# A three-block transformer kernel: in the first mixer, part of the shift row summed on VectorE, biases added by one-row products, constants loaded later

## The chip, the cores and the metric

The kernel is one program on one core of a Trainium2 chip. The metric is the device time in microseconds of one execution, as the median of several.

## The reference

Three different blocks are applied to x, 512 rows of 1024 numbers. The change lies in the start of the first one, which is, cut to what matters:

```python
mod = jax.nn.silu(c) @ w_ada + b_ada                     # 1024 -> 6 * 1024
shift1, scale1, gate1, shift2, scale2, gate2 = split(mod, 6)
h = rms_norm(x, norm1_w) * (1.0 + scale1) + shift1
proj = h @ w_in                                          # q, k, v, conv parts, index parts
...                                                      # selected attention, short convolution
x = x + gate1 * (y_mix @ w_out)
h2 = rms_norm(x, norm2_w) * (1.0 + scale2) + shift2
x = x + gate2 * peer_ffn(h2, ...)
```

The second block is a hybrid mixer with a mixture of experts, the third a hybrid attention layer; neither is touched.

## The kernel before

`first_mixer` does everything of the first block up to h2. The modulation has twelve half rows j of 512 columns (two for each of the six vectors), in the order `ADA_ORDER`: j = 0, 1 are scale1, j = 2, 3 are shift1, the others come later.

**Half rows 0 to 3** are products on TensorE (L661). The stationary operand is a column of silu(c) spread over 128 columns, the moving one a 128x512 part of w_ada, so each of the 128 rows of the PSUM bank `side[j % 2]` holds the same modulation row. Eight parts (k) make a half row; the parts of one half row come in two transfers of 1 MB (`ada_first`, semaphores `ada1_in`, eight in all). VectorE then adds the bias, which a broadcast transfer has put into `mod1` (L704 and L705 for scale1, with norm1_w; L708 for shift1).

**The rows.** ScalarE sums the squares of x (L754). VectorE multiplies the rows by the root and by scale1 (L714, four 128-row tiles) into `hn`, adds shift1 (L738), and TensorE transposes each tile in two halves of four 128x128 blocks (L774). ScalarE copies each half as its high part (L764), VectorE subtracts it for the low part (L743). After the eighth (`h_low` at 8) the weight products may start.

**Weight products.** `pieces` are the 128-column pieces of w_in (512 KB each). SP loads them into three buffers `raw` (L784), ScalarE rounds the high part (L813) and VectorE forms the low part (L821, `low_done`). TensorE makes 24 products of 512 columns a piece (L863), in eight groups k of three.

**Half rows 4 to 11** need pieces of 256 KB (`w_ada_later`, L647), through two buffers `ada_raw`; each piece q is multiplied by its column of silu(c) and accumulated on VectorE (L691 for the first of eight, L694 for the others, `ada_used`); a load waits until the piece two before it is used. One product with a matrix of ones (L672) then sums over the 128 rows, and VectorE adds the bias (L704, L705, L708).

**The index scores** of the attention (L1014 on TensorE, L1024 on ScalarE, L1036 and L1039 on VectorE, two buffers between each pair) start once six pieces of w_in are through; then VectorE selects the keys (L1050, L1055). The softmax lanes follow (L1095 to L1139), the output projection and h2.

**Order.** On each engine several Python generators yield between steps, and `weave_by` runs them in the order that `FIRST_ORDER` gives, written out as text: "c22" is 22 steps of the third program. Every engine executes its queue in order. For "sync" the programs are a `loads`, b `weights_in` and c `ada_in`; for "tensor" a `ada_tensor`, b `rows_tensor`, c `products`, e `rel_tensor`; for "scalar" a `rows_scalar`, b `rounded`; for "vector" a `ada_vector`, b `rows_vector`, c `rests`, f `rel_vector`. One step of `products` is one group of three products, eight make a piece; one step of `ada_vector` is one accumulation or the output after eight.

```python
def weave_by(order, *programs):
    for program in programs:
        next(program, None)
    for part in order.split():
        for _ in range(int(part[1:] or 1)):
            next(programs[ord(part[0]) - ord("a")], None)
```

`consts` is one 128-row tile of constants; its first 256 columns are the identity (`C["ident"]`) and the ones (`C["ones"]`).

## Time and profile before

| | us |
|---|---|
| median of 3 runs | 3362.2 |
| lowest and highest | 3358.63 and 3362.36 |
| profiled execution, its own time | 3367.17 |
| its span | 3365.4 |
| TensorE busy | 3012.6 (90%) |
| VectorE busy | 2430.1 (72%) |
| ScalarE busy | 1392.1 (41%) |
| GpSimd busy | 713.0 (21%) |

The span runs from the first instruction to the last of the profiled execution; its own time is what the same clock as that of the runs gave for it. Busy times are shares of the span. PE is TensorE, PEld its weight loads, DVE VectorE, ACT ScalarE, SPq the queue of SyncE that issues transfers. A matrix product in plain fp32 appears as two records. Ends of matmul records are modelled, so the distance between starts tells more than a duration.

### The profile page before, as it was taken

Reading aid. Unit: us, or ns where it says so; the run is one execution under the profiler, and the core shown is the slowest. Engines: PE = TensorE matmul, PEld = TensorE weight load, DVE = VectorE, ACT = ScalarE, POOL = GpSimd, SP = SyncE. Lnnn points to the kernel's source line nnn. Section 1 sums busy time; section 2 is a strip of 40 time slices with the busy share of each in tenths; the row PEclk is TensorE's granted clock in tenths of the full one; section 3 lists DMA queues with packets and bytes.
Section 4 is the critical chain, followed back from the end, with each engine's and each line's share of the span. In section 5 each row is a group of like instructions: output and inputs, shape, how many; then the busy total and the mean of one; then the engine's idle time right before and its main releaser. Section 6 shows DMA issues by size and latency. Waiting matters only on the chain. (4 is left out here: it accounts for less than half of the span.)

```text
span 3365.4 us, 35225 instructions
## 1 busy us (share of the span) xinstructions
PE 3012.6 (90%) x11968; PEld 1988.2 (59%) x11968; DVE 2430.1 (72%) x4830; ACT 1392.1 (41%) x2332; POOL 713.0 (21%) x583
## 2 busy tenths in 40 slices
PE   7999988887788777777789999999899999969999
PEld 4676633333333333333357898777788888857777
DVE  4888678777777777777759765555789888964665
ACT  2344222222222222222234333444588888853764
POOL 0000144444444444444410000000121222100000
PEclk9998989999988999999899999999999999989999
DMA  7423499999999999999962111343899999931112
GB/s 295 138 76 101 178 374 415 417 408 420 418 407 421 421 408 417 417 419 409 418 256 82 59 56 45 101 170 108 322 363 375 373 369 375 371 125 63 57 45 76
DMA packets 163767, 905.93 MB, mean 269 GB/s; under 512 B 27137, under 2 KB 27649, under 8 KB 71810
## 3 DMA queue, kind: packets, MB, share of 16 engines
q0 software_dynamic: 84000, 549.52, 39.8%
q1 hardware_dynamic: 79586, 354.11, 28.8%
q8 instruction: 100, 1.64, 0.2%
q14 instruction: 81, 0.66, 0.1%
HBM read 896.71 MB, written 31.99 MB: 276 GB/s over the span
## 5 line engine op out<-in xcount | busy, mean ns | idle before, releaser
L256 PE MATMUL peer_acc<-peer_uv,peer_diag 128*128 128x512 f32 x1952 | 959.3, 643 | 257.0 <-ACT peer_diag L308 254.6
L256 PEld LDWEIGHTS peer_acc<-peer_uv,peer_diag 128*128 128x128 f32 x1952 | 389.4, 205 | 806.2 <-issue 459.6
L435 DVE CUSTOM_DVE_ANT_0 peer_uv<-peer_uv,firsts_h 128x1024 f32<-128x1024 f32 x512 | 626.8, 1226 | 321.0 <-DMA peer_uv<-in_peer_uv,peer_experts 319.6
L213 POOL DMA_INDIRECT peer_uv<-in_peer_uv,peer_experts x512 | 590.2, 1153 | 1117.3 <-PE peer_acc L256 684.6
L3146 DVE TENSOR_TENSOR slotted_low<-slotted_raw,slotted_high 128x2048 fp32r<-128x2048 f32 x192 | 434.2, 2288 | 64.3 <-ACT slotted_high L3091 64.1
L3091 ACT ACTIVATE slotted_high<-slotted_raw 128x2048 fp32r<-128x2048 f32 x192 | 365.7, 1920 | 58.4 <-PE slotted_h L3044 47.8
L308 ACT ACTIVATE peer_diag<-all_consts,peer_weights 128x128 f32<-128x128 f32 x512 | 165.1, 390 | 313.6 <-DVE peer_weights L416 305.6
L299 ACT ACTIVATE peer_act_in<-peer_act_in 128x4 f32<-128x4 f32 (+2 forms) x131 | 26.8, 205 | 628.5 <-DVE peer_act_in L435 628.5
L3044 PE MATMUL slotted_h<-slotted_high,slotted_xT_high 128*128 128x512 f32 x512 | 203.1, 397 | 0.6 <-DVE slotted_xT_low L3153 0.6
L3044 PE MATMUL slotted_h<-slotted_high,slotted_xT_low 128*128 128x512 f32 x512 | 200.2, 391 | 0.0
L3044 PE MATMUL slotted_h<-slotted_low,slotted_xT_high 128*128 128x512 f32 x512 | 199.6, 390 | 0.0
L1821 PE MATMUL mixers_acc<-mixers_xT_high,mixers_high 128*128 128x512 f32 x448 | 192.0, 429 | 3.2 <-DVE mixers_low L1842 3.2
L1821 PE MATMUL mixers_acc<-mixers_xT_low,mixers_high 128*128 128x512 f32 x448 | 176.0, 393 | 0.0
L1821 PE MATMUL mixers_acc<-mixers_xT_high,mixers_low 128*128 128x512 f32 x448 | 175.5, 392 | 0.0
L2911 POOL MEMSET slotted_xg<- 128x1024 f32 x1 | 1.0, 952 | 639.4 <-POOLq L3317 639.4
L3006 POOL DMA_INDIRECT results<-slotted_ob,slotted_rows_out x32 | 32.3, 1009 | 451.9 <-ACT slotted_ob L3118 451.9
L1842 DVE TENSOR_TENSOR mixers_low<-mixers_raw,mixers_high 128x1024 fp32r<-128x1024 f32 (+1 forms) x77 | 93.1, 1209 | 40.9 <-ACT mixers_high L1835 40.1
L1835 ACT ACTIVATE mixers_high<-mixers_raw 128x1024 fp32r<-128x1024 f32 (+1 forms) x77 | 80.6, 1046 | 101.0 <-PE mixers_acc L1821 76.2
L3044 PEld LDWEIGHTS slotted_h<-slotted_high,slotted_xT_low 128*128 128x128 f32 x512 | 96.1, 188 | 21.1
L3044 PEld LDWEIGHTS slotted_h<-slotted_high,slotted_xT_high 128*128 128x128 f32 x512 | 96.1, 188 | 20.9 <-issue 0.7
L3044 PEld LDWEIGHTS slotted_h<-slotted_low,slotted_xT_high 128*128 128x128 f32 x512 | 96.3, 188 | 19.0
L863 PE MATMUL firsts_acc<-firsts_hT_high,firsts_high 128*128 128x512 f32 (+1 forms) x240 | 105.4, 439 | 1.8 <-DVE firsts_hT_low L743 1.8
(786 smaller groups left out, 5694.2 us busy)
## 6 DMA issues: line engine op xcount, KB each, us to landing
slotted_raw<-in_moe_w SPq DMA_DIRECT2D x192, 1024.0 KB, 7.3
mixers_raw<-in_w_in SPq DMA_DIRECT2D x56, 512.0 KB, 3.3
firsts_ada_raw<-in_w_ada_later SPq DMA_DIRECT2D x64, 256.0 KB, 2.7
third_raw<-in_w_in SPq DMA_DIRECT2D x30, 512.0 KB, 3.3
firsts_raw<-in_w_in SPq DMA_DIRECT2D x28, 512.0 KB, 3.5
firsts_ada_first<-in_w_ada_first SPq DMA_DIRECT2D x8, 1024.0 KB, 18.0
peer_uv<-in_peer_uv,peer_experts POOLq DMA_INDIRECT x512, 11.3
ffn_w_raw<-in_peer_wq SPq DMA_DIRECT2D x10, 512.0 KB, 8.4
```

The costliest lines, as they stand in the source:

```text
L213: pool.indirect_dma_start(uv[:, n % R, :, :].rearrange("p a d -> p (a d)"), None, A["peer_uv"], bass.IndirectOffsetOnAxis(ap=experts[:, si ...
L256: mm = nc.tensor.matmul(acc[t % 2][j][:, :], diag[:, n % 4, :], uv[:, n % R, 1, j * BANK:(j + 1) * BANK], start=(n == first), stop=(m == E ...
L308: nc.scalar.activation(diag[:, n % 4, :], C["ident"], ACT.Copy, scale=weights[:, side, i:i + 1])\
L435: nc.vector.tensor_tensor_reduce(uv[:, n % R, 0, :], uv[:, n % R, 0, :], h2[:, t, :], 1.0, 0.0, ALU.mult, ALU.add, act_in[:, side, i:i + 1 ...
L863: mm = nc.tensor.matmul(bank[rows, :], b, a, start=(k == 0 and r == 0), stop=(k == KD - 1 and r == 2))
L1821: mm = nc.tensor.matmul(bank[:, :], b, a, start=(k == 0 and r == 0), stop=(k == piece["kb"] - 1 and r == 2))
L1835: nc.scalar.activation(high[:, p % 2, 0:size], raw[:, p % RAW, 0:size], ACT.Copy).then_inc(high_done, 1)
L1842: nc.vector.tensor_tensor(low[:, p % 2, 0:size], raw[:, p % RAW, 0:size], high[:, p % 2, 0:size].bitcast(F32), ALU.subtract).then_inc(low_ ...
L3006: pool.indirect_dma_start(results, bass.IndirectOffsetOnAxis(ap=rows_out[:, e:e + 1], axis=0), ob[:, e % 2, :], None, bounds_check=2 * L - ...
L3044: mm = nc.tensor.matmul(ps_h[i // 2][:, :], a, b, start=(k == 0 and r == 0), stop=(k == KD - 1 and r == 2))
L3091: nc.scalar.activation(high[:, p % RING, :], raw[:, p % RAW, :], ACT.Copy).then_inc(high_done, 1)
L3146: nc.vector.tensor_tensor(low[:, p % RING, :], raw[:, p % RAW, :], high[:, p % RING, :].bitcast(F32), ALU.subtract).then_inc(low_done, 1)
```

## The change

Half rows 0 to 3 get their bias from a product with one row of ones as the stationary operand and the bias row as the moving one (`bias_row`, 8 KB), so the 1 MB broadcast into `mod1` is gone, and each output is one VectorE operation. Of half row 2 the first four parts are multiplied and summed on VectorE (`SUMMED`), and one product with ones adds the sum. Only the first 256 columns of the constants are loaded early, the others after the first weight pieces. Weight pieces 0 to 2 are all loaded behind the modulation pieces; before, piece 0 was first and 1 and 2 came behind later loads. `idle_products` multiplies ones with the identity into a bank that the next transposes overwrite: six before each tile, eight before the first weight product. The low part of weight piece 0 moves behind the first two row additions. The accumulations for half rows 4 to 6 all move behind the rows phase, and their ones products (L672) from 2, 24 and 45 groups of weight products to 20, 36 and 49.

```python
def idle_products(nc, C, bank, n):
    for _ in range(n):
        nc.tensor.matmul(bank[:, 0:P], C["ones"], C["ident"], start=True, stop=True)
```

```diff
--- before.py
+++ after.py
@@ -525,6 +525,7 @@
         acc_first, acc_last = arena.at(152 * KB + 128, "acc_first", [P, 2, BANK]), arena.at(0, "acc_last", [P, 2, BANK])
         ada_raw, tsq = arena.at(164 * KB + 128, "ada_raw", [P, 2, BANK]), arena.at(168 * KB + 128, "tsq", [P, 4, P])
         norm_row = arena.at(170 * KB + 128, "norm_row", [P, D])
+        bias_row = arena.at(156 * KB + 128, "bias_row", [P, 2 * D])
         w1_at = {2: 136, 3: 144, 0: 152, 1: 160}
         w1 = {kp: (arena.at(a * KB, f"w1_high{kp}", [P, 2, BANK], F32R), arena.at((a + 4) * KB, f"w1_low{kp}", [P, 2, BANK], F32R))
               for kp, a in w1_at.items()}
@@ -598,6 +599,8 @@
         c_ready, ada_done, ada_used, ada_out, gate2_out = (st.sem(n) for n in ("c_ready", "ada_done", "ada_used", "ada_out",
                                                                                "gate2_out"))
         ada_chain, eps_ready = st.sem("ada_chain"), st.sem("eps_ready")
+        square_in, bias_in, shift_used = st.sem("square_in"), st.sem("bias_in"), st.sem("shift_used")
+        SQUARE, SUMMED = 2 * P, 4
         FIRST = 32
 
         def ada_key(q):
@@ -605,6 +608,9 @@
 
         def ada_acc(j):
             return (acc_first if j < 4 + FIRST // 8 else acc_last)[:, j % 2, :]
+
+        def tile_of_bias(j):
+            return slice(COLS[j], COLS[j] + BANK)
 
         def mod_row(j):
             half = slice(BANK * (j % 2), BANK * (j % 2) + BANK)
@@ -619,13 +625,13 @@
                 j, kh = divmod(n, 2)
                 sp_queue.dma_start(ada_first[:, n], A["w_ada_first"][j, kh]).then_inc(ada1_in[n], 16)
                 if n == 0:
+                    sp_queue.dma_start(C["all"][:, 0:SQUARE], A["consts"][:, 0:SQUARE]).then_inc(square_in, 16)
+                    sp_queue.dma_start(bias_row[0:1, :], A["b_ada"][:, 0:2 * D]).then_inc(bias_in, 16)
                     sp_queue.dma_start(norm_row[:, :], A["norm1_w"].broadcast_to([P, D])).then_inc(rows_in, 16)
-                    sp_queue.dma_start(mod1[:, :, :], A["b_ada"][:, 0:2 * D].rearrange("o (a n) -> o a n", a=2)
-                                       .broadcast_to([P, 2, D])).then_inc(rows_in, 16)
                 if 1 <= n <= 4:
                     sp_queue.dma_start(x[:, n - 1, :], A["x"][tile(n - 1), :]).then_inc(x_in[n - 1], 16)
-            sp_queue.dma_start(C["all"], A["consts"]).then_inc(consts_in, 16)
             yield -60.0
+            sp_queue.dma_start(C["all"][:, SQUARE:], A["consts"][:, SQUARE:]).then_inc(consts_in, 16)
             for dst, name in ((cw[:, :, :], "conv_w_col"), (cb[:, :], "conv_b_col"), (cgain[:, :], "conv_norm_col"),
                               (qk_gain[:, :], "qk_norm_cols")):
                 sp_queue.dma_start(dst, A[name]).then_inc(small_in, 16)
@@ -655,12 +661,20 @@
             for j in range(4):
                 if j >= 2:
                     pe.wait_ge(ada_out, j - 1)
-                for k in range(KD):
+                direct = range(SUMMED if j == 2 else 0, KD)
+                for k in direct:
                     if k % 4 == 0:
                         pe.wait_ge(ada1_in[2 * j + k // 4], 16)
-                    mm = nc.tensor.matmul(side[j % 2][:, :], c_col[:, k:k + 1].broadcast_to([P, P]),
-                                          ada_first[:, 2 * j + k // 4, k % 4, :], start=(k == 0), stop=(k == KD - 1))
-                mm.then_inc(ada_done, 1)
+                    nc.tensor.matmul(side[j % 2][:, :], c_col[:, k:k + 1].broadcast_to([P, P]),
+                                     ada_first[:, 2 * j + k // 4, k % 4, :], start=(k == direct[0]), stop=False)
+                if j == 2:
+                    pe.wait_ge(shift_used, SUMMED)
+                    nc.tensor.matmul(side[0][:, :], C["ones"], ada_acc(2), start=False, stop=False)
+                if j == 0:
+                    pe.wait_ge(square_in, 16)
+                    pe.wait_ge(bias_in, 16)
+                nc.tensor.matmul(side[j % 2][:, :], C["ones"][0:1, :], bias_row[0:1, tile_of_bias(j)], start=False, stop=True)\
+                  .then_inc(ada_done, 1)
             for j in range(4, N_ADA):
                 yield ada_key(8 * (j - 3) - 1) + 1.5
                 if j == 4:
@@ -678,7 +692,8 @@
             for j in range(N_ADA):
                 if j < 4:
                     yield -190.0
-                    dve.wait_ge(rows_in, 32)
+                    if j == 0:
+                        dve.wait_ge(rows_in, 16)
                 else:
                     for k in range(KD):
                         q = 8 * (j - 4) + k
@@ -698,7 +713,12 @@
                     dve.wait_ge(mod_in, 64)
                 dve.wait_ge(ada_done, j + 1)
                 dst, bank = mod_row(j), side[j % 2][:, :]
-                if j < 2 or j in (6, 7):
+                if j < 2:
+                    nc.vector.scalar_tensor_tensor(dst, bank, 1.0, norm_row[:, BANK * j:BANK * j + BANK], ALU.add, ALU.mult)\
+                      .then_inc(ada_out, 1)
+                elif j < 4:
+                    nc.vector.tensor_copy(dst, bank).then_inc(ada_out, 1)
+                elif j in (6, 7):
                     if j == 6:
                         dve.wait_ge(norm2_in, 16)
                     chain(nc.vector.scalar_tensor_tensor(dst, bank, 1.0, dst, ALU.add, ALU.add))
@@ -707,6 +727,16 @@
                 else:
                     nc.vector.tensor_tensor(dst, bank, dst, ALU.add).then_inc(ada_out, 1)
                 if j == 1:
+                    dve.wait_ge(c_ready, 1)
+                    dve.wait_ge(ada1_in[4], 16)
+                    for k in range(SUMMED):
+                        part = ada_first[:, 4, k, :]
+                        if k == 0:
+                            ins = nc.vector.tensor_scalar(ada_acc(2), part, c_col[:, 0:1], None, ALU.mult)
+                        else:
+                            dve.wait_ge(shift_used, k)
+                            ins = nc.vector.scalar_tensor_tensor(ada_acc(2), part, c_col[:, k:k + 1], ada_acc(2), ALU.mult, ALU.add)
+                        ins.then_inc(shift_used, 1)
                     dve.wait_ge(rooted, 1)
                     chain(nc.vector.reciprocal(sums[:, :], sums[:, :]))
                     dve.wait_ge(ada_out, 2)
@@ -767,8 +797,8 @@
             for n in range(2 * NT):
                 t, half = divmod(n, 2)
                 yield row_key(t, 6) + 0.5 * half
-                if n == 0:
-                    pe.wait_ge(consts_in, 16)
+                if half == 0:
+                    idle_products(nc, C, all_banks[n], 6)
                 pe.wait_ge(rows_normed, t + 1)
                 for b in range(4):
                     tr = nc.tensor.transpose(all_banks[n][:, tile(b)], hn[:, t, tile(4 * half + b)], C["ident"])
@@ -828,7 +858,10 @@
                 size = piece["kb"] * piece["w"]
                 wh, wl = (b[:, p % 2, 0:size].rearrange("p (k n) -> p k n", k=piece["kb"]) for b in (high, low))
                 if p == 0:
+                    pe.wait_ge(h_low, 2)
+                    idle_products(nc, C, big[0], 8)
                     pe.wait_ge(h_low, 2 * NT)
+                    pe.wait_ge(consts_in, 16)
                 if name == "out":
                     kp = KP[m]
                     if m == 0:
@@ -4203,20 +4236,20 @@
 FIRST_ORDER = {
     "sync": (
-        "b a c2 a c4 b c b c b c a c5 b c3 b c5 b c3 b c2 b c3 b c3 b c3 b c b3 c b4 c b2 c b c b3 c b c b2 c3 b "
+        "a b3 c2 a b c3 b a c3 b c2 b c4 b c4 b c12 b c3 b c3 b c b3 c b4 c b2 c b c b3 c b c b2 c3 b "
...
     "tensor": (
-        "a b8 c2 a c22 a c21 e2 a c4 d e2 c e2 c2 e2 c e c e c e4 c e2 c e2 c e2 c a e2 c2 e2 c8 d c5 d c5 d c7 d "
+        "a b8 c20 a c16 a c9 e2 c4 a d e2 c e2 c2 e2 c e c e c e4 c e2 c e2 c e2 c a e2 c2 e2 c8 d c5 d c5 d c7 d "
...
     "scalar": (
-        "b a9 b c b c b2 c b c b c f2 c b f12 b f2 c f8 b e c2 b2 e c b c e c b c b2 c e2 b c b c2 b c e b c b c "
+        "a b a8 b c b c b2 c b c b c f2 c b f12 b f2 c f8 b e c2 b2 e c b c e c b c b2 c e2 b c b c2 b c e b c b c "
...
     "vector": (
-        "a c a4 b2 a2 b3 a b2 a b a b2 a b2 a5 c a2 c a2 c a5 c a c a5 c a d a2 e f4 c f2 a f a f3 a f2 a f2 a f3 "
+        "a5 b2 c b10 a3 c a3 c a2 c a5 c a4 c a5 c a5 d a2 e f4 c f2 a f a f3 a f2 a f2 a f3 "
...
```

## Rows read from the trace of the kernel before

**Rows 1.** The page's header, whole execution.
```profile
span 3365.4 us, 35225 instructions
```

**Rows 2.** Windows: busy us and instructions of each engine, granted clock, DMA share, GB/s.
```profile
49.00:62.00 13.00, 8.23 (x20) 5.45 (x21) 8.64 (x13) 2.76 (x5) 0.00 (x0) 0.50 0.80 284
...
310.00:332.00 22.00, 18.25 (x60) 11.16 (x59) 18.71 (x31) 12.71 (x22) 0.00 (x0) 0.61 0.16 48
200.00:300.00 100.00, 99.28 (x472) 68.86 (x468) 80.57 (x199) 43.71 (x102) 0.00 (x0) 1.00 0.30 98
```

**Rows 3.** Timeline, opening: start us, us, engine, line, operation [idle before].
```profile
5.15 1.23 DVE L821 TENSOR_TENSOR firsts_low<-firsts_raw,firsts_high 128x1024 fp32r<-128x1024 f32 x1 [4.27 <-ACT firsts_high L813]
...
8.77 17.74 PE L661 MATMUL firsts_side<-firsts_ada_first,firsts_c_col 128*128 128x512 f32 x32 [8.77 <-DMA firsts_ada_first<-in_w_ada_first]
9.75 0.34 PEld L661 LDWEIGHTS firsts_side<-firsts_ada_first,firsts_c_col 128*128 128x128 f32 x1 [0.52 <-issue]
10.61 0.34 PEld L661 LDWEIGHTS firsts_side<-firsts_ada_first,firsts_c_col 128*128 128x128 f32 x1 [0.52 <-issue]
...
19.05 0.30 PEld L661 LDWEIGHTS firsts_side<-firsts_ada_first,firsts_c_col 128*128 128x128 f32 x2 [0.88 <-DMA firsts_ada_first<-in_w_ada_first]
...
26.67 14.23 PE L661 MATMUL firsts_side<-firsts_ada_first,firsts_c_col 128*128 128x512 f32 x32 [0.16 <-DMA firsts_ada_first<-in_w_ada_first]
...
30.34 0.30 PEld L661 LDWEIGHTS firsts_side<-firsts_ada_first,firsts_c_col 128*128 128x128 f32 x2 [0.82 <-DMA firsts_ada_first<-in_w_ada_first]
...
41.01 0.69 DVE L708 TENSOR_TENSOR firsts_mod<-firsts_side,firsts_mod 128x512 f32<-128x512 f32 x1 [4.70 <-PE firsts_side L661]
```

**Rows 4.** DMA issues of the first 60 us: KB each, median us to landing.
```profile
firsts_ada_first<-in_w_ada_first SPq DMA_DIRECT2D x8, 1024.0 KB, 18.0
...
all_x<-in_x SPq DMA_DIRECT2D x4, 512.0 KB, 16.1
...
firsts_mod<-in_b_ada SPq DMA_DIRECT2D x1, 1024.0 KB, 10.1
```

**Rows 5.** Timeline, rows phase.
```profile
41.74 2.36 DVE L738 TENSOR_TENSOR firsts_hn<-firsts_hn,firsts_mod 128x1024 f32<-128x1024 f32 x2
...
44.60 0.75 DVE L694 SCALAR_TENSOR_TENSOR firsts_acc_first<-firsts_ada_raw,firsts_c_col,firsts_acc_first 128x512 f32<-128x512 f32 x1
...
51.39 1.97 PE L774 MATMUL firsts_side<-all_consts,firsts_hn 128*128 128x128 f32 x8 [2.56 <-DVE firsts_hn L738]
...
53.77 1.28 DVE L743 TENSOR_TENSOR firsts_hT_low<-firsts_side,firsts_hT_high 128x512 fp32r<-128x512 f32 x2
```

**Rows 6.** Timeline, TensorE, weight products and L672.
```profile
55.20 0.76 PE L863 MATMUL firsts_acc<-firsts_hT_high,firsts_high 128*128 128x512 f32 x1 [1.84 <-DVE firsts_hT_low L743]
...
58.64 2.04 PE L672 MATMUL firsts_side<-firsts_acc_first,all_consts 128*128 128x512 f32 x2 [0.54 <-DVE firsts_acc_first L694]
...
62.78 0.40 PE L863 MATMUL firsts_acc<-firsts_hT_high,firsts_high 128*128 128x512 f32 x1
...
92.36 1.12 PE L672 MATMUL firsts_side<-firsts_acc_first,all_consts 128*128 128x512 f32 x2
...
99.10 0.50 PE L863 MATMUL firsts_acc<-firsts_hT_high,firsts_high 128*128 128x512 f32 x1
```

**Rows 7.** Timeline, VectorE, accumulations and the output after them.
```profile
61.40 0.48 DVE L691 TENSOR_SCALAR firsts_acc_first<-firsts_ada_raw,firsts_c_col 128x512 f32<-128x512 f32 x1
...
64.62 0.75 DVE L694 SCALAR_TENSOR_TENSOR firsts_acc_first<-firsts_ada_raw,firsts_c_col,firsts_acc_first 128x512 f32<-128x512 f32 x1 [0.62 <-DMA firsts_ada_raw<-in_w_ada_later]
...
90.55 1.60 DVE L694 SCALAR_TENSOR_TENSOR firsts_acc_first<-firsts_ada_raw,firsts_c_col,firsts_acc_first 128x512 f32<-128x512 f32 x2 [2.28 <-DMA firsts_ada_raw<-in_w_ada_later]
...
93.59 0.69 DVE L704 SCALAR_TENSOR_TENSOR firsts_mod<-firsts_side,firsts_mod 128x512 f32<-128x512 f32 x1 [0.30 <-issue]
```

**Rows 8.** Line L647, 76 to 80 us: later modulation pieces, to landing.
```profile
DMA to landing us min/median/max: 2.6/2.8/2.9
```

**Rows 9.** Waits of VectorE, 96 to 330 us.
```profile
DVE firsts_probs L1130 <- PE firsts_mid L1095: 9.4, 16, 1.5
```

## The prediction

> **What bounds the kernel.** I began with the page's header, for the profiled execution's own time: a span of 3365.4 us [rows 1] inside 3367.2 us measured, so 1.8 us lie around it. That execution is 5.0 us above the 3362.2 us median of the runs. All sums below are made against 3367.2 and then lowered by 5.0. The change touches only the first mixer, so next I read windows of its first 420 us. In the middle of it (200 to 300 us) TensorE is busy 99.28 of 100 us while VectorE is busy 80.57 [rows 2]: whatever makes TensorE's weight products start sooner should shift everything behind them, if nothing else holds them. Two stretches show a granted clock near 0.5, that is 1.2 GHz: 49 to 62 us, and part of 310 to 332 us. The change can reach the first.
>
> The timeline of the opening shows three steps. First, modulation pieces of 1 MB arrive and are multiplied with c (L661): TensorE waits for pieces at 19.05 and 30.34 us, three intervals of 3.76 us [rows 3]. Each interval holds one 1024 KB piece and one 512 KB tile of x [rows 4], 1.57 MB, so the transfers run at 418 GB/s and pace the opening. Second, VectorE alone carries the rows phase from 41.74 to 55.05 us (53.77 + 1.28) [rows 5]: row additions (L738), low halves (L743), and between them accumulations of later modulation pieces (L691/L694). TensorE is mostly idle there. Third, the weight products (L863) begin at 55.20 us, at half clock [rows 6]. They have passed 12 products by 62.78.
>
> **The opening.** Ahead of the second piece the change takes away the 1024 KB bias broadcast, and it puts weight piece 0 (512 KB) behind the pieces. It adds 128 KB of constants and 8 KB of bias. Net 1400 KB less, 1.43 MB / 0.418 = 3.4 us earlier for every piece from the second on; the first gains the 512 KB alone, 1.25 us, plus 0.2 us of issue, and lands for a start near 7.3 instead of 8.77. From there TensorE itself is the bound. A product is two records; records stand 0.86 us apart at first (loads at 9.75 and 10.61) and 14.23/32 = 0.44 later [rows 3]. So: four slow products 6.9, four fast 3.45, the bias product 0.86: first row done at 18.5; nine more products, 7.75: 26.2. The shift row's four direct products wait for piece six (30.34 - 3.4 = 26.9) and end at 30.4. VectorE's sum starts after the second row's output, 26.2 + 0.7, and takes 0.48 + 3 x 0.75 and gaps of 0.1 us, 3.0 in all [rows 5, 7]: 29.9, so it is hidden with 0.5 us to spare (if late, its overrun falls on TensorE directly). Ones and bias products bring 32.1, the last nine 39.9. The output op starts at 40.0 instead of 41.01: **1.0 us gained**. So four bias products and one ones product (5 x 0.86) against four saved ones eat most of the transfer gain. The removed L705s and the copy instead of L708 lie in VectorE's idle time, but for the last copy: 0.
>
> **The rows phase.** VectorE has four row additions at 1.18 (2.36 for two), eight low halves at 0.60 (1.28 for two, whose records overlap; counted 1.2), the low half of weight piece 0 at 1.15, moved here from 5.15 us where it was free, and about 0.3 waiting for the last tile's transposes. The six accumulations that lie in it now (0.58 + 5 x 0.67 = 3.9) are gone. From the first addition at 40.8: 40.8 + 4.7 + 4.8 + 1.15 + 0.3 = 51.8, first product at 52.0 instead of 55.20: **3.2 us gained**, the 1.0 above included. The ones products in the waits: a transpose of the same 128 columns takes 1.97/8 = 0.25 us at half clock, half of that at full; a quarter of the 0.86 us of a 512-column product of this kind is 0.22 us. So six take 0.8 to 1.3 us, and the eight before piece 0 take 1.1 to 1.7 us. A tile comes every 2.4 us and its eight transposes take 1.1, so they fit; the last eight end between 51.4 and 52.0. I take 0, upper bound 0.3.
>
> **The clock.** TensorE was busy for bits of 41 to 49 us and then had 0.50 granted until 62 [rows 2]. With the ones products it hardly idles from 40 to 52 us, so I take full clock. Between 62.78 and 92.36 us lie 123 products, one L672 and two score products (1.5 us): (29.58 - 1.5)/123 = 0.228 each. Twelve at that and an L672 at 0.93 need 3.7 us, where now 7.58 go by (with a 0.54 wait for VectorE inside): **3.9 us gained**. Lead at that point: 7.1 us. Bounds: 0 (clock stays low) to 3.9. The Trainium skill, page "TensorE: Matmul & The Clock Gate", section "What's actually happening", says the default is the low clock and that activity releases it; by that rule the ones products would earn the whole 3.9, and the sum would be the same. The rows say only that sparse narrow work was not enough.
>
> **What takes the lead back.** The 24 accumulations of rows four to six of the modulation now all start after the rows phase, at 52.0; until now six were done by 54. They run through two buffers: a transfer is issued when its buffer is read, so a pair costs landing plus one operation. The landing is 2.6 to 2.9 us [rows 8] for 256 KB, where 418 GB/s would need 0.6: it is the delay, not the bandwidth. The Trainium skill, page "DMA: Bandwidth & Descriptors", section "Anatomy of one DMA — SWDGE (gpsimd) path", gives about 2.0 us fixed per transfer, for another issuing engine than SP; by it the landing would be 2.6 us, as in the row, and it speaks against packing these transfers into less time.
>
> Floor: q0 at 52.0, 11 pairs at 3.4 (61.40 to 64.62 was 3.2, with the short first op) and the last pair's 1.5: 90.9. Now the 16 from 61.40 to 92.15 take 1.92 each, with waits for weight pieces and their transfers between them [rows 7]; 24 at that, less one landing, give 95.4. In between, 11 x 3.4, two waits for TensorE before the modulation outputs (1.5 and 1.3, for buffers read late) and raw pieces ahead of some transfers: I take 93.7, against 92.15 now. TensorE wants the third L672 after 49 groups of three products (0.68) and two L672: 52.0 + 33.3 + 1.9 + 0.6 = 87.8. So it waits: about 2 us at the second L672, the rest at the third, and in order behind it stand all products and the score products. After it VectorE's output (L704) starts at 93.7 + 0.1 + 0.93 + 0.1 = 94.8 instead of 93.59, 1.2 us late. The order from there is the same in both kernels. VectorE then feeds the scores (L1036/L1039) without a gap and TensorE's score products wait on them through ScalarE; the product group now at 99.10 becomes 1.0 us late (0.4 of slack less, and 0.2 of small waits more). With both engines 1 us late, the end of the mixer is 1.0 us late. Bounds from the chain's ends: -1.8 and +2.7. Later stages see the same work.
>
> Moving constants and weights 1 and 2: the constants land near 41 us, the masks are wanted after 96; cover is large. Weights 1 and 2 now precede the accumulations' transfers, no cost. Weight piece 3 waits on SP for piece 0's low half at 44.5: wanted only at 68. The sum: 3367.2 - 7.1 + 8.1 = 3368.2, less 5.0: **3363.2 us** (+0.03%). A measurement of this kernel tells about 0.2%, 6.7 us.
>
> **Rivals.** (A) The accumulations keep up, because transfers land sooner in quieter queues or TensorE's waits fall where VectorE had slack: the whole lead stays, 3362.2 - 7.1 = 3355.1; half of it 3358.6. For it: VectorE idles 9.4 us on TensorE's scores later [rows 9], so its lateness may be absorbed; against it: no landing below 2.5. (B) Slower: the wait before the third L672, up to 5 us with little work, drops the clock as at 49 us. As then for 13 us at half, 6.6 us of products are lost: 3363.2 + 6.6 = 3369.8. It decides if this wait is as empty as the idle times between 41 and 49 us were, and if it does cost all of that. The Trainium skill, page "TensorE: Matmul & The Clock Gate", section "HAM oscillation — how this bites in real kernels", describes just such a loss after waits for transfers. (C) The ones products don't hold the clock: the first 12 products lose the 3.9, the second L672 finds its data ready later, and the third follows 3 to 4 us behind: 3367. (D) The opening is not shortened, as transfers share engines otherwise than in order: 1 us more.
>
> **How the numbers follow.** The sum with its own range 3359.5 to 3366: 0.5. A: 0.22, half of it beyond 0.2%. B: 0.1, C: 0.13, D: 0.05. The range 3354.5 to 3369 leaves out the far side of A and most of B. Noise of the later transfer-bound stages moves some of A and the sum over the line: faster 0.18, same 0.7, slower 0.12.
>
> **What would show it.** L708's successor at 40 us, the first L863 near 52 with a granted clock of 1.00, TensorE waiting for acc_first before the second and third L672, the third done near 94.8, and the scores at the old times plus 1. A third L672 done by 91 speaks for A; a window of 90 to 105 us with 0.5 to 0.8 granted for B. The prediction is wrong if the chain of accumulations is faster than 1.6 us each.

## The result, and the profile after

The changed kernel takes 3374.2 us (median of 7 runs, 3370.5 to 3377.6), the kernel before 3361.6 (7 runs beside them): ratio 1.003, 95% interval 1.002 to 1.004. The medians are 12.6 us apart; the interval of the ratio allows 7 to 13 us. The forecast was 3363.2, with a range up to 3369. The profiled execution of after took 3370.53 us, the fastest of its seven, and that of before was 5.0 us above its median. So these two differ by only 3.4 us, and I go by positions inside the first mixer rather than by spans.

The window table of after answers to [rows 2]. Columns as there.

```profile
28.00:30.00 2.00, 2.00 (x3) 0.77 (x3) 1.96 (x4) 0.00 (x0) 0.00 (x0) 0.50 0.96 401
41.00:49.00 8.00, 7.49 (x62) 6.74 (x61) 7.45 (x9) 2.35 (x5) 0.00 (x0) 1.00 0.72 275
49.00:62.00 13.00, 13.00 (x78) 11.39 (x76) 8.34 (x12) 4.48 (x7) 0.00 (x0) 1.00 0.42 122
62.00:92.00 30.00, 24.93 (x98) 17.89 (x97) 14.65 (x20) 5.37 (x8) 0.00 (x0) 0.94 0.64 194
99.00:110.00 11.00, 8.75 (x21) 4.76 (x22) 7.41 (x15) 1.53 (x4) 0.00 (x0) 0.50 0.33 99
```

From 49 to 62 us the granted clock is 1.00 where it was 0.50: the ones products hold it (run 2 below, without them, has 0.65). Then TensorE stands still for 5 of the 30 us from 62 to 92, and from 99 to 110 us it runs at half clock.

The timeline of after, opening, answers to [rows 3] (L668 is L661 of before, L672 here the new ones product for the shift sum, L676 the bias product, L720 the copy in place of L708):

```profile
6.50 8.88 PE L668 MATMUL firsts_side<-firsts_ada_first,firsts_c_col 128*128 128x512 f32 x16 [6.50 <-DMA firsts_ada_first<-in_w_ada_first]
...
26.09 5.37 PE L668 MATMUL firsts_side<-firsts_ada_first,firsts_c_col 128*128 128x512 f32 x8 [1.55 <-DMA firsts_ada_first<-in_w_ada_first]
...
27.76 0.34 PEld L668 LDWEIGHTS firsts_side<-firsts_ada_first,firsts_c_col 128*128 128x128 f32 x1 [0.51 <-issue]
28.61 0.34 PEld L668 LDWEIGHTS firsts_side<-firsts_ada_first,firsts_c_col 128*128 128x128 f32 x1 [0.52 <-issue]
...
32.25 1.12 PE L676 MATMUL firsts_side<-firsts_bias_row,all_consts 1*128 1x512 f32 x2
33.30 7.13 PE L668 MATMUL firsts_side<-firsts_ada_first,firsts_c_col 128*128 128x512 f32 x16
...
41.52 0.69 DVE L720 COPY firsts_mod<-firsts_side 128x512 f32<-128x512 f32 x1 [7.42 <-PE firsts_side L676]
```

TensorE starts 2.3 us earlier, then waits 1.55 us for a piece, loses its clock (weight loads 0.85 apart), and the last output comes 0.5 us later than before, not 1.0 earlier.

The timeline of after from 52 to 105 us, rows of VectorE, TensorE and SP's queue (L706 and L709 are the accumulations, L686 the ones product L672 of before, L728 and L724 the outputs L708 and L704, L851 a low half, L896 the weight products, L653 and L814 the loads):

```profile
52.99 0.48 DVE L706 TENSOR_SCALAR firsts_acc_first<-firsts_ada_raw,firsts_c_col 128x512 f32<-128x512 f32 x1
53.13 0.50 PE L896 MATMUL firsts_acc<-firsts_hT_high,firsts_high 128*128 128x512 f32 x1
...
58.02 0.33 SPq L814 DMA_DIRECT2D firsts_raw<-in_w_ik  x1
58.40 0.43 SPq L642 DMA_DIRECT2D firsts_norm_row<-in_norm_w  x1
58.87 7.30 SPq L653 DMA_DIRECT2D firsts_ada_raw<-in_w_ada_later  x3
...
65.06 0.75 DVE L709 SCALAR_TENSOR_TENSOR firsts_acc_first<-firsts_ada_raw,firsts_c_col,firsts_acc_first 128x512 f32<-128x512 f32 x1 [4.67 <-DMA firsts_ada_raw<-in_w_ada_later]
65.73 1.22 DVE L851 TENSOR_TENSOR firsts_low<-firsts_raw,firsts_high 128x1024 fp32r<-128x1024 f32 x1
66.87 0.75 DVE L709 SCALAR_TENSOR_TENSOR firsts_acc_first<-firsts_ada_raw,firsts_c_col,firsts_acc_first 128x512 f32<-128x512 f32 x1
...
67.00 0.50 PE L896 MATMUL firsts_acc<-firsts_hT_high,firsts_high 128*128 128x512 f32 x1 [2.69 <-DVE firsts_low L851]
...
72.60 0.69 DVE L728 TENSOR_TENSOR firsts_mod<-firsts_side,firsts_mod 128x512 f32<-128x512 f32 x1 [2.25 <-PE firsts_side L686]
73.20 0.48 DVE L706 TENSOR_SCALAR firsts_acc_first<-firsts_ada_raw,firsts_c_col 128x512 f32<-128x512 f32 x1
...
83.93 0.75 DVE L709 SCALAR_TENSOR_TENSOR firsts_acc_first<-firsts_ada_raw,firsts_c_col,firsts_acc_first 128x512 f32<-128x512 f32 x1 [2.11 <-DMA firsts_ada_raw<-in_w_ada_later]
...
85.77 1.10 PE L686 MATMUL firsts_side<-firsts_acc_first,all_consts 128*128 128x512 f32 x2 [2.38 <-DVE firsts_acc_first L709]
...
87.59 0.48 DVE L706 TENSOR_SCALAR firsts_acc_first<-firsts_ada_raw,firsts_c_col 128x512 f32<-128x512 f32 x1
...
98.19 0.75 DVE L709 SCALAR_TENSOR_TENSOR firsts_acc_first<-firsts_ada_raw,firsts_c_col,firsts_acc_first 128x512 f32<-128x512 f32 x1 [1.23 <-DMA firsts_ada_raw<-in_w_ada_later]
99.58 0.75 DVE L709 SCALAR_TENSOR_TENSOR firsts_acc_first<-firsts_ada_raw,firsts_c_col,firsts_acc_first 128x512 f32<-128x512 f32 x1 [0.64 <-DMA firsts_ada_raw<-in_w_ada_later]
100.48 2.05 PE L686 MATMUL firsts_side<-firsts_acc_first,all_consts 128*128 128x512 f32 x2 [3.90 <-DVE firsts_acc_first L709]
...
102.62 0.69 DVE L724 SCALAR_TENSOR_TENSOR firsts_mod<-firsts_side,firsts_mod 128x512 f32<-128x512 f32 x1 [2.29 <-PE firsts_side L686]
```

This is the loss, as far as the profile shows it. The weight products begin 2.1 us sooner than in [rows 6], but the 24th accumulation ends at 100.3 (99.58 + 0.75) and the output L724 starts at 102.62, against 93.59 in [rows 7]: 9.0 us late. The same lateness stands at the end of the mixer, in the tile view of the closing weights, where L843 starts at 355.2 and L813, its counterpart of before, at 346.0:

```profile
L843 ACT ACTIVATE firsts_w_high<-firsts_raw x4: 1042/1052/1062, 355.2 to 361.9; 128x1024 fp32r<-128x1024 f32 x4
```

```profile
L813 ACT ACTIVATE firsts_w_high<-firsts_raw x4: 1042/1052/1061, 346.0 to 352.7; 128x1024 fp32r<-128x1024 f32 x4
```

### The profile page after: what moved, and what is told of

Its sections match the earlier page's. It is cut to its first block and busy times, and to the rows that moved or that the text cites. A ratio compares the mean times of both kernels' runs of the same rounds, so it can differ in the third digit from the quotient of the medians.

```text
span 3368.8 us, 35358 instructions
## 1 busy us (share of the span) xinstructions
PE 3022.6 (90%) x12034; PEld 1993.0 (59%) x12034; DVE 2431.8 (72%) x4832; ACT 1390.2 (41%) x2331; POOL 708.6 (21%) x583
## 5 line engine op out<-in xcount | busy, mean ns | idle before, releaser
L896 PE MATMUL firsts_acc<-firsts_hT_high,firsts_high 128*128 128x512 f32 (+1 forms) x240 | 104.4, 435 | 2.7 <-DVE firsts_low L851 2.7
```

The source lines that it names most:

```text
L896: mm = nc.tensor.matmul(bank[rows, :], b, a, start=(k == 0 and r == 0), stop=(k == KD - 1 and r == 2))
```

## The experiments

Times in this table are the first row addition, the first weight product, the output L724 (or its counterpart), the first rounding of the closing weights, and the median with its ratio to the kernel before on the same chip. Experiments are told apart by ratio and position: the kernel before had medians of 3362.6 beside 1 to 4, 3363.4 beside 5 to 8, 3362.6 beside 9 to 11 and 3361.2 beside 12. The ratio is the recorded one of the runs beside each other; it is not exactly the quotient of the two medians.

The positions come from one profiled execution of each kernel, and some of their differences are chance. The opening has the same code in after and in 1, 2, 3, 4 and 7, and the row addition starts at 42.25 to 43.15 there, in 7 at 44.86. With the opening of before it starts at 41.74, 42.45 and 42.09 (before, 5, 11). Behind the closing weights all kernels have the same code, and the profiled spans leave 3012.6 (5) to 3019.4 us (before, 4, 11) for it. So a shift of 9 us stands out in the positions, one of 1 or 2 us doesn't.

| | row add. | first product | output | closing | median | ratio, 95% interval |
|---|---|---|---|---|---|---|
| before | 41.74 | 55.20 | 93.59 | 346.0 | 3361.6 | 1 |
| after | 42.25 | 53.13 | 102.62 | 355.2 | 3374.2 | 1.003, 1.002 to 1.004 |
| 1 early sums | 43.15 | 57.66 | 94.04 | 344.6 | 3362.5 | 1.0000, 0.9991 to 1.0009 |
| 2 no ones | 42.46 | 54.09 | 104.46 | 358.4 | 3375.8 | 1.0037, 1.0023 to 1.0050 |
| 3 four buffers | 43.05 | 53.93 | 94.35 | 347.7 | 3364.7 | 1.0007, 0.9998 to 1.0017 |
| 4 ones before third | 42.97 | 53.84 | 102.21 | 355.3 | 3376.7 | 1.0046, 1.0030 to 1.0061 |
| 5 before plus ones | 42.45 | 55.83 | 94.96 | 344.8 | 3365.8 | 1.0006, 0.9997 to 1.0015 |
| 6 early sums, no shift sum | 42.47 | 56.98 | 93.56 | 346.3 | 3363.3 | 0.9996, 0.9986 to 1.0005 |
| 7 four buffers, issued early | 44.86 | 55.74 | 92.92 | 345.4 | 3362.2 | 0.9997, 0.9988 to 1.0006 |
| 8 as 7, no shift sum | 42.24 | 53.12 | 90.31 | 343.0 | 3362.1 | 0.9989, 0.9980 to 0.9998 |
| 9 as 8, earlier L672 | 41.47 | 52.35 | 91.64 | 344.3 | 3363.6 | 1.0003, 0.9994 to 1.0012 |
| 10 as 8, no biases | 38.67 | 49.55 | 86.72 | 338.8 | 3358.5 | 0.9989, 0.9980 to 0.9998 |
| 11 late sums alone | 42.09 | 52.68 | 101.49 | 354.3 | 3374.2 | 1.0030, 1.0020 to 1.0041 |
| 12 late broadcasts | 37.57 | 48.45 | 85.62 | 337.9 | 3356.5 | 0.9984, 0.9975 to 0.9993 |

**1. The accumulations back in their old places.** In the changed kernel the orders of SP, TensorE and VectorE are, from the rows phase on, those of before, but for the first three weight pieces, which SP still loads early (one of the three shown).

```diff
     "vector": (
-        "a5 b2 c b10 a3 c a3 c a2 c a5 c a4 c a5 c a5 d a2 e f4 c f2 a f a f3 a f2 a f2 a f3 "
+        "a5 b2 c a2 b3 a b2 a b a b2 a b2 a5 c a2 c a2 c a5 c a c a5 c a d a2 e f4 c f2 a f a f3 a f2 a f2 a f3 "
```

> The changed kernel with only the written orders put back for the accumulations and the ones products L672: the accumulations lie between the row additions again and the third L672 comes after 45 groups instead of 49. Theory 1 (the deferred accumulations make a chain through two buffers that ends late and holds both engines): the third L672 runs near 93 us instead of 100.5, and the first load of the closing weights (firsts_w_high) starts near 344 to 347 us, where the changed kernel has 355.2 and the kernel before 346.0; the time is 9 to 12 us below the changed kernel's. Rival 2 (the opening with its bias products, or the ones products in the waits, cost the time): it stays at 352 or later and within 3 us of the changed kernel.

It takes back all of the loss (ratio 1.0000; 11.7 us between the medians), though the first product comes 4.5 us later than in after: late accumulations are dearer than a late start. The closing weights of this kernel:

```profile
L843 ACT ACTIVATE firsts_w_high<-firsts_raw x4: 1044/1055/1062, 344.6 to 351.3; 128x1024 fp32r<-128x1024 f32 x4
```

**2. No ones products.** From the changed kernel:

```diff
-                if half == 0:
-                    idle_products(nc, C, all_banks[n], 6)
...
-                    pe.wait_ge(h_low, 2)
-                    idle_products(nc, C, big[0], 8)
```

> The changed kernel without the ones products in the waits before the transposes and before the first weight product. Theory 1: the clock falls near 49 us as before the change and the first products lose up to 3.9 us, but the third L672 still waits for the accumulations, which start no later, so closing weights start at 355 to 359 us: 0 to 4 us slower than the changed kernel. Rival 2 (the ones products delay the rows phase by more than their clock brings): first weight product 0.5 us or more earlier and closing weights before 354.

The clock falls again (0.65 granted from 49 to 62 us) and the closing weights come 3.2 us later than in after. So the ones products are not the cause of the loss, and by the positions they gain something. The time can't tell it: 1.0037 (1.0023 to 1.0050) and the 1.003 of after are not apart.

**3. Four buffers for the 24 accumulations.** From the changed kernel; a load waits for the piece four before it.

```diff
+                elif q >= 4:
+                    sp_queue.wait_ge(ada_used, q - 3)
                 j, k = 4 + q // 8, q % 8
-                sp_queue.dma_start(ada_raw[:, q % 2, :], A["w_ada_later"][j - 4, k]).then_inc(ada2_in[q % 2], 16)
+                sp_queue.dma_start(ada_buf(q), A["w_ada_later"][j - 4, k]).then_inc(ada2_in[q % (4 if q < FIRST else 2)], 16)
```

> The changed kernel with four buffers instead of two for the first 32 later modulation pieces, each load issued when the piece four before it is used; every order as in the changed kernel. Theory 1: the pace of the chain is landing delay through two buffers, so with four it goes from 2.0 us to about 1.5 us an accumulation, the third L672 runs at 90 to 94 instead of 100.5 us, and closing weights start 6 to 9 us earlier than 355.2. Rival 3 (the chain is held by VectorE's own order or by bandwidth): less than 3 us earlier.

The timeline of VectorE in this kernel (L725 the accumulation, L740 the output):

```profile
63.25 0.75 DVE L725 SCALAR_TENSOR_TENSOR firsts_acc_first<-firsts_ada_raw,firsts_c_col,firsts_acc_first 128x512 f32<-128x512 f32 x1 [4.62 <-DMA firsts_ada_raw<-in_w_ada_later]
...
91.11 1.61 DVE L725 SCALAR_TENSOR_TENSOR firsts_acc_first<-firsts_ada_more,firsts_c_col,firsts_acc_first 128x512 f32<-128x512 f32 x2
94.35 0.69 DVE L740 SCALAR_TENSOR_TENSOR firsts_mod<-firsts_side,firsts_mod 128x512 f32<-128x512 f32 x1 [1.63 <-PE firsts_side L702]
```

The last accumulation ends at 92.7 instead of 100.3, with the same pieces and the same arithmetic; only the moments of issue differ. Buffers waiting for a landing set the pace of most of the chain. One wait they don't explain: the piece q5 is still issued behind a weight piece and the norm2 row, and VectorE still stands at it for 4.62 us (4.67 in after). With the later pieces issued earlier, in run 7, that wait is gone.

**4. Ones products in the wait before the third L672.** From the changed kernel:

```diff
+                if j == 6:
+                    pe.wait_ge(ada_used, 8 * (j - 3) - 2)
+                    idle_products(nc, C, side[j % 2], 10)
```

> The changed kernel with ten more ones products ahead of the third L672, once six of its eight accumulations are done, so that TensorE is not idle in that wait. Theory 1: VectorE's late chain sets what follows, so keeping the clock brings at most the 2 to 3 us that TensorE loses at half clock between 99 and 110 us, and closing weights start at 352 to 355 us. Rival 4 (the fall of the clock after the wait is most of the loss): they start before 351 us.

Windows of this kernel, and below them its timeline:

```profile
92.00:100.00 8.00, 7.68 (x44) 4.36 (x42) 4.89 (x6) 2.19 (x4) 0.00 (x0) 1.00 0.47 142
99.00:110.00 11.00, 7.63 (x29) 4.72 (x29) 8.58 (x16) 1.54 (x4) 0.00 (x0) 0.82 0.37 110
```

```profile
100.98 1.13 PE L689 MATMUL firsts_side<-firsts_acc_first,all_consts 128*128 128x512 f32 x2 [1.21 <-DVE firsts_acc_first L712]
```

The ones product now takes 1.13 instead of 2.05 us, and 0.82 instead of 0.50 is granted behind it. Yet the closing weights come at 355.3, as in after, just outside what I expected. The clock lost in this wait costs nothing that the positions show: TensorE's next wait, 2.16 us before its scores at 106.14, is for ScalarE, which itself had waited for VectorE.

**5. The ones products alone, in the kernel before.**

```diff
+                if half == 0:
+                    idle_products(nc, C, all_banks[n], 6)
...
+                    pe.wait_ge(h_low, 2)
+                    idle_products(nc, C, big[0], 8)
```

> The kernel before, with nothing but the ones products added (six before each tile's transposes, eight before the first weight product). Theory 1: the clock stays at 2.4 GHz from 49 to 62 us, 12 products and an L672 gain up to 3.9 us, but the third L672 (92.36 us before) has its accumulations at 92.15 and moves little, so TensorE waits there instead and the closing weights start at 343 to 346 us (346.0 before): 0 to 3 us gained. Rival 5 (what the clock gives back is kept): 342.5 or earlier.

The granted clock in the window from 49 to 62 us rises from 0.50 to 0.92, the closing weights come 1.2 us earlier, which a single profile can't show, and the time is the same within the interval. The gained clock is given back at the first L672, where TensorE waits 2.9 us for accumulations that did not become faster.

**6. As 1, without the shift sum.**

```diff
-        SQUARE, SUMMED = 2 * P, 4
+        SQUARE, SUMMED = 2 * P, 0
...
-                if j == 2:
-                    pe.wait_ge(shift_used, SUMMED)
-                    nc.tensor.matmul(side[0][:, :], C["ones"], ada_acc(2), start=False, stop=False)
```

> The run with early accumulations (e1), and all eight parts of half row 2 on TensorE again, nothing of it summed on VectorE. Theory: in the changed kernel TensorE has nothing between 24.5 and 26.1 us and then runs four products at half clock (2.0 us); with parts 0 to 3 in that hole the wait and the low clock are gone, four products (3.4 us) replace wait, low clock and one ones product (1.5 + 2.0 + 0.9), and the first row addition starts 0.5 to 1.5 us earlier than 43.15. Rival (the sum on VectorE does save TensorE's time): it starts 1 to 3 us later.

The row addition moves from 43.15 to 42.47 and the time stays within its interval: the shift sum gains nothing here. The closing weights come 1.7 us later than in run 1, no more than the positions scatter.

**7. As 3, with the later pieces issued earlier on SP.**

```diff
-        "a b3 c2 a b c3 b a c3 b c2 b c4 b c4 b c12 b c3 b c3 b c b3 c b4 c b2 c b c b3 c b c b2 c3 b "
+        "a b3 c2 a c2 b c3 b c3 b a c2 b c4 b c4 b c4 b c9 b c3 b c b3 c b4 c b2 c b c b3 c b c b2 c3 b "
```

> The changed kernel with four buffers, and SP's written order changed so that pieces 2 and 3 are loaded during the rows phase and later ones ahead of the weight pieces by as many steps as the buffers allow. VectorE's and TensorE's orders stay those of the changed kernel. Theory 1: the accumulations no longer wait for landings, the third L672 stands at 87 to 91 us and no L672 waits for more than 1 us; the closing weights start at 341 to 345 us and the time is 2 to 5 us below the kernel before. Rival 3 (VectorE's order holds them): third L672 at 92 or later, closing weights at 347 or later.

No L672 waits any more, and the closing weights come at 345.4 although the first product is 1.8 us later than in run 3. Both are just short of what I expected: 341 to 345 us, and a time 2 to 5 us lower, where the ratio is 0.9997. The lateness of the first product is from the opening, whose code is that of run 3, so I take it for chance. It shows in this kernel's timeline and, below it, its window (the four direct products in 6.6 us, at 0.66):

```profile
27.44 6.63 PE L684 MATMUL firsts_side<-firsts_ada_first,firsts_c_col 128*128 128x512 f32 x8 [2.25 <-DMA firsts_ada_first<-in_w_ada_first]
```

```profile
24.00:34.00 10.00, 7.75 (x12) 3.11 (x12) 8.30 (x10) 3.14 (x5) 0.00 (x0) 0.66 1.01 415
```

**8. As 7, without the shift sum** (the edit of 6).

> As the run with four buffers issued early, and half row 2 wholly on TensorE. If both theories hold, the effects add: closing weights another 0.5 to 1.5 us earlier than in that run, and the time 3 to 6 us below the kernel before.

The row addition comes at 42.24, 2.6 us earlier, and the closing weights 2.4 us earlier, where I expected 0.5 to 1.5; part of that is the slow opening of run 7's profile. All that TensorE waits for from 50 to 120 us, in the view of its waits (us in total, times, longest):

```profile
PE firsts_mid L1060 <- ACT firsts_rel L1070: 2.7, 2, 2.1
```

The output comes at 90.31, 3.3 us before that of the kernel before, and so do the closing weights (343.0 against 346.0).

**9. As 8, with the first two L672 earlier in TensorE's order.**

```diff
-        "a b8 c20 a c16 a c9 e2 c4 a d e2 c e2 c2 e2 c e c e c e4 c e2 c e2 c e2 c a e2 c2 e2 c8 d c5 d c5 d c7 d "
+        "a b8 c15 a c14 a c16 e2 a c4 d e2 c e2 c2 e2 c e c e c e4 c e2 c e2 c e2 c a e2 c2 e2 c8 d c5 d c5 d c7 d "
```

> The run with four buffers and no shift sum, and the three L672 after 15, 29 and 45 groups of weight products instead of 20, 36 and 49, since their accumulations are done early there (63.2, 76.3 and 88.0 us) and VectorE waited for TensorE. If what follows hangs on VectorE's output behind the third L672, that output starts at 87 to 88 us instead of 90.3, TensorE's wait at the scores (2.7 us) shrinks below 1 us, and the closing weights start at 339.5 to 341.5 us instead of 343.0. Rival (the scores are held by TensorE's products): 342.5 or later.

A miss: the second and third L672 then wait 4.3 us together for their accumulations (2.58 and 1.70), and the closing weights come at 344.3. In VectorE's order low halves stand between the accumulations. One of them stands 1.80 us for ScalarE's high half at 59.71 us, and by the code a high half waits until TensorE is through with the piece two before. So the chain can't run far ahead of the products; that this is what held it is argued from the code, not shown by a run.

**10. As 8, without the one-row products** (shift1 and scale1 get no bias).

```diff
-                nc.tensor.matmul(side[j % 2][:, :], C["ones"][0:1, :], bias_row[0:1, tile_of_bias(j)], start=False, stop=True)\
-                  .then_inc(ada_done, 1)
+                mm.then_inc(ada_done, 1)
```

> The run with four buffers and no shift sum, with the four bias products left out (the biases of shift1 and scale1 are not added at all). It shows what they cost on TensorE: if TensorE's own work sets the opening, the first row addition starts 3.5 to 4.2 us earlier than 42.24 (four products with their gaps, 1.05 each). If the transfers set it, less than 1.5 us earlier. A gain there should reach the closing weights only in part.

The row addition moves from 42.24 to 38.67, 3.6 us for four products, and the closing weights by 4.2. The ratio is that of run 8 all the same; these two intervals are too wide to show such a step.

**11. The late accumulations alone.** Run 5 with orders like those of after (one of the three shown).

```diff
     "vector": (
-        "a c a4 b2 a2 b3 a b2 a b a b2 a b2 a5 c a2 c a2 c a5 c a c a5 c a d a2 e f4 c f2 a f a f3 a f2 a f2 a f3 "
+        "a c a4 b12 a3 c a3 c a2 c a5 c a4 c a5 c a5 d a2 e f4 c f2 a f a f3 a f2 a f2 a f3 "
```

> The kernel before plus the ones products (e5), with nothing else of the change but the written orders that put the accumulations behind the rows phase and the three L672 after 20, 36 and 49 groups. Opening, biases and constants are those of the kernel before. Theory 1: this alone makes the loss: third L672 at 99 to 102 us, closing weights at 353 to 357 us, 8 to 11 us above the kernel before. Rival 2 (the new opening is needed for it): below 350.

It gives the whole result without the opening's changes: 11.6 us between the medians, ratio 1.003. The closing weights of this kernel:

```profile
L815 ACT ACTIVATE firsts_w_high<-firsts_raw x4: 1043/1052/1062, 354.3 to 361.2; 128x1024 fp32r<-128x1024 f32 x4
```

 TensorE's waits from 50 to 120 us in this kernel have the pattern of after (L686 6.3 us in two waits, L896 2.7 us in one):

```profile
PE firsts_side L672 <- DVE firsts_acc_first L694: 6.7, 2, 3.8
PE firsts_acc L867 <- DVE firsts_low L823: 2.5, 1, 2.5
```

**12. As 8, the biases again by VectorE, from broadcasts queued late.** The x tiles stand behind the weight pieces 1, 2, 4 and 5 (`n`), and the first later pieces no longer wait for `ada_done`.

```diff
+                if n == 3:
+                    sp_queue.dma_start(mod1[:, 1, :], A["b_ada"][:, D:2 * D].broadcast_to([P, D])).then_inc(bias_in, 16)
+                if n == 7:
+                    sp_queue.dma_start(C["all"][:, 0:SQUARE], A["consts"][:, 0:SQUARE]).then_inc(square_in, 16)
+                    sp_queue.dma_start(mod1[:, 0, :], A["b_ada"][:, 0:D].broadcast_to([P, D])).then_inc(shift_in, 16)
...
-                nc.tensor.matmul(side[j % 2][:, :], C["ones"][0:1, :], bias_row[0:1, tile_of_bias(j)], start=False, stop=True)\
-                  .then_inc(ada_done, 1)
```

> The changed kernel with the accumulations through four buffers and issued early, no shift sum on VectorE (as in e8), and no one-row products: the biases of shift1 and scale1 are added by VectorE as before, from broadcasts that are queued late, scale1's behind the fourth weight piece and shift1's behind the eighth, with the x tiles between the pieces. The whole computation is done. Theory that the one-row products hold the opening (e10, without them, had the row addition at 38.67 against 42.24): row addition at 38 to 39.5 us, first product of the rows at 49 to 50.5, closing weights at 338.5 to 341 (e8: 343.0), time 3 to 7 us below the kernel before. Rival, that the transfers set the opening as soon as TensorE has less to do (the broadcasts of 512 KB stand before the pieces again): row addition at 41 us or later, closing weights within 2 us of 343.0, time as e8.

Timeline of this kernel (L687 the modulation products, L777 the row addition, L907 the first weight product):

```profile
6.17 30.64 PE L687 MATMUL firsts_side<-firsts_ada_first,firsts_c_col 128*128 128x512 f32 x64 [6.17 <-DMA firsts_ada_first<-in_w_ada_first]
...
37.57 2.36 DVE L777 TENSOR_TENSOR firsts_hn<-firsts_hn,firsts_mod 128x1024 f32<-128x1024 f32 x2
...
48.45 0.50 PE L907 MATMUL firsts_acc<-firsts_hT_high,firsts_high 128*128 128x512 f32 x1
```

TensorE multiplies all 32 modulation parts in one go, with no wait for a piece: the transfers don't set this opening. All three positions are a little earlier than I expected. This is the fastest version: 3356.5 against 3361.2 us, 0.16% faster (0.07% to 0.25%).

## Why the prediction was wrong

**The step that failed** is "what takes the lead back": the term "q23 done at 93.7 (bounds 90.9 to 95.4)". It was done at 100.3. Its mechanism was right: two buffers, the landing sets the pace, TensorE waits at the second and third L672. Its size was not. The 6.6 us divide so, from the timeline of after:

- The start: 52.99 instead of 52.0, 1.0 us.
- Three pairs of the first row: 13.9 us (52.99 to 66.87) instead of 10.2, 3.7 us. Piece q5 was issued at 58.87, behind a weight piece and the norm2 row, 512 KB each, and landed after 6.2 us. The same view gives 2.8 to 3.0 us for two others:

```profile
DMA to landing us min/median/max: 6.2/6.2/6.2
...
DMA to landing us min/median/max: 2.8/2.9/3.0
```

- The last pair of the first row and the turn to the second: 6.3 us (66.87 to 73.20) instead of 4.9, 1.4 us. VectorE stood at that late piece for 4.67 us, with the low half of weight piece 2 behind it in its order; TensorE therefore waited 2.69 us, and so L686, L728 and the next accumulations were late too. The two chains delay each other.
- The rest: the pairs of the second and third row took 3.58 (73.20 to 83.93, three) and 3.53 us instead of 3.4, 0.9 us together; the last pair 2.14 instead of 1.5, 0.6 us; the last pair of the second row with the turn to the third (83.93 to 87.59) 3.66 instead of 4.7, 1.0 us less.

The prediction's 2.8 us above its floor were the two waits for TensorE at the turns; the "raw pieces ahead of some transfers" got nothing, and the norm2 row isn't named. By run 3 the late q5 is the queue's part of the miss, which more buffers alone leave in place; the slow pace of the rest is the buffers' part: the second and third row together took 27.1 us in after (73.20 to 100.33) and 22.9 with four buffers. Its upper bound took one landing off 24 accumulations at the 1.92 us of [rows 7]. Without that deduction, and from the true start, the pace gives 52.99 + 24 x 1.92 = 99.1; the chain went at 1.97 (47.3/24).

By the Trainium skill, page "DMA: Bandwidth & Descriptors", section "Queues, rings and completion order", each DMA engine takes the descriptors of an issuing queue in ring order. An estimate by that rule is 1.31 MB at 418 GB/s, 3.1 us, and the 2.2 us by which a lone landing exceeds its bandwidth time: 63.3 when counted from the issue at 58.02, where the trace has 65.06. The rule agrees in kind: the weight piece landed 4.7 us after its issue (62.7), the norm2 row at 64.3 and q5 at 65.1. Of the other 1.8 us, some 0.8 is the rate, since from 60 to 64 us the windows of after show 328 to 340 GB/s and not 418; the rest stays open.

**From there to the end.** Behind q23 I had 1.1 us to the output; it was 2.3, as L686 ran at half clock. Predicted lateness at the output 1.2, measured 9.0; at the mixer's end 1.0, measured 9.2. So "both engines late, the end is late by as much" held. Runs 1 and 11 show the cause: moving only the accumulations, with their loads and their L672, takes it away and brings it. The later places of L672 alone don't cost it, since runs 3 and 7 keep them. Whether anything more was lost behind the closing weights isn't shown: 9.2 us lie inside the 7 to 13 us of the measurement, and the profiles differ by up to 6.8 us there (3012.6 to 3019.4 us).

**The opening** was to gain 1.0 us and lost 0.5. The transfers came sooner, as worked out (6.50 and 26.09 us; I had 7.3 and 26.9). TensorE's side was mis-sized: it was through with the second row at 24.5, not 26.2, and waited 1.55 us for the piece behind. I had counted four slow products, as in [rows 3]; here the weight loads are 0.85 apart only up to 10.04 us, and the eight products took 8.88 us, not 10.35. The clock then fell to 0.50, so the four direct products took 5.2 us instead of 3.5. Each bias product cost 1.05 us, not 0.86 (32.25 to 33.30). The shift sum on VectorE was hidden, as predicted, but it opened the very gap in which the clock falls: with it 0.66 to 0.83 was granted from 24 to 34 us in all six profiles of this opening, without it (6, 8, 9) 1.00, and the row addition came at 41.47 to 42.47 instead of 42.25 to 44.86. The mean difference is 1.1 us; the 2.6 us of 8 against 7 rest on the one slow opening of 7.

**The rows phase** was to take 11.2 us from the first addition to the first product (40.8 to 52.0) and took 10.9 (42.25 to 53.13): right.

**The clock** was worth 3.9 us by the sum. It was held at 1.00, as predicted. Run 2, without the ones products, has its closing weights 3.2 us later, 1.0 us of which is its later first product. In the kernel before (run 5) most of the gain is given back in a wait for accumulations.

**The rivals.** A (the chain keeps up) is refuted. B forecast the right side for a reason that carries nothing: the clock did fall behind the third wait, as the page "TensorE: Matmul & The Clock Gate" of the Trainium skill, section "HAM oscillation — how this bites in real kernels", describes it after waits for transfers, and the trace agrees (0.50 from 99 to 110 us). But run 4 kept most of it and gained nothing that shows. C is refuted by the window from 49 to 62 us. D's outcome came true, worse than priced (no 1.0 us gained, 0.5 lost), but not for its reason: the transfers came in time, and TensorE took longer. Even the two together, 3363.2 + 6.6 + 1, stay below what came.

**Where the parts stand.** The idea of an earlier start is sound if the accumulations can follow: with four buffers, issued early, the same late order costs nothing (7), without the shift sum it has 3.0 us at the closing weights (8), and without one-row products another 5.1 (12). In time, 7 is the same as the kernel before, 8 is barely clear of it (0.9980 to 0.9998), and 12 is clear (0.9975 to 0.9993).

## What to carry to other kernels

A chain of small transfers through two buffers has a price per operation that its own rows in the trace show (1.92 us here for 0.75 us of work). When such a chain is moved, multiply that by its length and take nothing off, and count every large transfer that its queue issues between. Before work is deferred to let a bottleneck engine start sooner, ask whether that engine's later steps wait for the deferred work; if so, the buffers come first. An engine with spare time in the mean (TensorE in this opening) may still set a stretch, and a product put there to save a transfer costs its full time (0.9 us each in run 10).

## What was not expected of the hardware

- A product with one row as stationary operand is no cheaper than one with 128: 1.05 us from its start to that of the next (32.25 to 33.30), and 3.6 us for the four that run 10 leaves out (0.9 each), while a 128-row product takes 0.86 from start to start (two records, 0.43 apart) and 0.89 with its end (7.13/8).
- After an idle time of 1.55 us between dense products, the granted clock went to 0.50, 1.7 us after they had begun again (loads 0.42 apart at 27.02 and 0.85 at 28.61). It was 0.50 from 27.4 to 30.4 us and 1.00 from 30.6 us.
- Ten ones products kept the clock across a wait of 3.7 us (97.30 to 100.98 in run 4), at no cost to the wait: L689 started when its data was there.
- The same opening code gave row additions from 42.25 to 44.86 us in six profiled executions, and the same code behind the closing weights took 3012.6 to 3019.4 us.
